# Raw inputs transposed ahead of their norm, with gains and row scales applied afterwards, in a two-layer decoder trunk

## The reference

```python
for i in range(2):
    h = rms_norm(x, attn_norm[i])
    x = x + (swa_sink_attention(h, ...) if i == 0 else stick_breaking_attention(h, ...))
    h = rms_norm(x, ffn_norm[i])
    x = x + (swiglu(h, ...) if i == 0 else moe_swiglu(h, ...))
return rms_norm(x, final_norm)
```

## Time and profile before

| | us |
|---|---|
| median of 3 runs | 1397.66 (1396.64 to 1399.08) |
| the profiled execution | 1399.92 |
| its span | 1398.10 |
| TensorE busy | 1379.1 (99%) |
| VectorE busy | 1091.6 (78%) |
| ScalarE busy | 922.9 (66%) |
| experts, from their first product | from 430.18 |

### The profile page before, as it was taken

The page is one execution under the profiler, slowest core; times in us unless marked ns, Lnnn a source line. Parts: engine busy times, 40 slices in busy tenths (PEclk is TensorE's granted clock), DMA queues, the critical chain, the costliest instruction groups (busy, mean ns, idle before and its releaser), DMA issues.

```text
span 1398.1 us, 19292 instructions
## 1 busy us (share of the span) xinstructions
PE 1379.1 (99%) x7165; PEld 1160.8 (83%) x7165; DVE 1091.6 (78%) x824; ACT 922.9 (66%) x762; POOL 43.3 (3%) x38
## 2 busy tenths in 40 slices
PE   9999999999999999999999999999999999999997
PEld 6879999889887888888888888888888888888885
DVE  5964444464548888988988898888888888889886
ACT  5754333445456777777777777777777777778775
POOL 2100000000000000000100000010000000000000
PEclk9999999999999999999999999999999999999999
DMA  9446553744327999999999999999999999999993
GB/s 324 156 162 206 190 181 122 247 159 158 114 91 292 385 368 358 389 387 371 369 394 374 353 395 389 359 376 394 380 349 394 386 361 373 390 372 359 392 372 124
DMA packets 185102, 430.48 MB, mean 308 GB/s; under 512 B 7047, under 2 KB 12241, under 8 KB 185058
## 3 DMA queue, kind: packets, MB, share of 16 engines
q1 hardware_dynamic: 181344, 417.36, 81.8%
q0 software_dynamic: 2896, 10.03, 2.6%
q10 hardware_dynamic: 818, 2.47, 0.6%
HBM read 422.48 MB, written 7.36 MB: 307 GB/s over the span
## 4 chain that ended last, share of the span: by engine, by line
PE 90%; DVE 5%; DMA 2%; issue 1%; ACT 1%; DVEq 0%; ACTq 0%; POOLq 0%
PE bank L1354 87%; DVE low L533 2%; DMA sum_dram<-qT,slot_row 2%; PE bank L1731 2%; DVE h L984 1%; PE bank L1700 0%; PE bank L1406 0%; PE bank L1515 0%; DMA qT<-in_onehot 0%; DVE work L1275 0%; DVE inT_low L1020 0%; DVE peak L1077 0%; DVE h L1067 0%; DVE work L1067 0%; DVE slot_spare L1281 0%
## 5 line engine op out<-in xcount | busy, mean ns | idle before, releaser
L533 DVE TENSOR_TENSOR low<-raw,high 128x2048 fp32r<-128x2048 f32 (+1 forms) x397 | 898.8, 2276 | 216.4 <-ACT high L528 214.2
L528 ACT CAST high<-raw 128x2048 fp32r<-128x2048 f32 (+1 forms) x397 | 754.8, 1903 | 298.5 <-PE bank L1354 295.2
L1354 PE MATMUL bank<-high,inT_high 128*128 128x512 f32 x1000 | 394.8, 395 | 4.4 <-DVE low L533 2.8
L1354 PE MATMUL bank<-high,inT_low 128*128 128x512 f32 x1000 | 389.9, 390 | 0.0
L1354 PE MATMUL bank<-low,inT_high 128*128 128x512 f32 x1000 | 389.5, 390 | 0.0
L1354 PEld LDWEIGHTS bank<-high,inT_high 128*128 128x128 f32 x1000 | 187.8, 188 | 45.7 <-DVE low L533 5.9
L1354 PEld LDWEIGHTS bank<-high,inT_low 128*128 128x128 f32 x1000 | 187.7, 188 | 39.9
L1354 PEld LDWEIGHTS bank<-low,inT_high 128*128 128x128 f32 x1000 | 187.9, 188 | 37.5
L1354 PE MATMUL bank<-high,hid_high 128*128 128x512 f32 x528 | 207.2, 392 | 0.0
L1354 PE MATMUL bank<-high,hid_low 128*128 128x512 f32 x528 | 205.7, 390 | 0.0
L1354 PE MATMUL bank<-low,hid_high 128*128 128x512 f32 x528 | 205.5, 389 | 0.0
(11 more groups left out here) (180 smaller groups left out, 644.2 us busy)
## 6 DMA issues: line engine op xcount, KB each, us to landing
raw<-in_moe_w_gate SPq DMA_DIRECT2D x112, 1024.0 KB, 7.0
raw<-in_moe_w_up SPq DMA_DIRECT2D x112, 1024.0 KB, 7.2
raw<-in_moe_w_down SPq DMA_DIRECT2D x112, 1024.0 KB, 6.9
raw<-in_sb_w_qkv SPq DMA_DIRECT2D x12, 1024.0 KB, 5.3
raw<-in_ffn_w_down SPq DMA_DIRECT2D x11, 1024.0 KB, 4.9
raw<-in_ffn_w_gate SPq DMA_DIRECT2D x10, 1024.0 KB, 5.7
raw<-in_ffn_w_up SPq DMA_DIRECT2D x10, 1024.0 KB, 5.1
raw<-in_swa_w_qkv SPq DMA_DIRECT2D x4, 1024.0 KB, 12.1
```

The lines of the kernel that those rows point to most:

```text
L528: nc.scalar.copy(high[n % SPLIT][:, :, 0:c], raw[r][:, :, 0:c]).then_inc(high_done, 1)
L533: nc.vector.tensor_tensor(low[n % SPLIT][:, :, 0:c], raw[n % RAW][:, :, 0:c], high[n % SPLIT][:, :, 0:c].bitcast(F32), ALU.subtract).then_ ...
L1354: return nc.tensor.matmul(out, lhsT, rhs, start=start, stop=stop, **kw)
```

## The change

The inputs of kv, of the dense layer and of q1 are now transposes of x itself. The gain, which by then lies along partitions, is multiplied in when the banks are evicted (`gained_part_high`, `gained_part_low`); the row scale is applied to the results: to k, v and q of layer 0, to the gate block ahead of Silu (up's factor is applied where the down product is added to x), and to q, k and v of layer 1. Where tokens lie along the free axis, the scales are spread over partitions by a matmul of ones with a diagonal. The transposes of each half of the features are issued as soon as x has that half, inside the products around; squares, roots and reciprocals follow behind them in `late_norm`. The last dense block is ordered by halves of the output. All gains and biases of the columns come in by three loads and one transpose. In `sb_sums` two matmuls become one.

```diff
@@ PSUM banks @@
-    transposed("hT1", (5, 0, 2, 1))
+    transposed("hT1", (5, 2, 3, 7))
+    u.use(("R", 1), 6)
@@ POOL @@
-            pool.dma_start(bias_tiles[:, :], a["swa_b_qkv"][0].rearrange("(t p) -> t p", p=P)).then_inc(biases_loaded, 16)
...
@@ ScalarE @@
+            act.dma_start(ident, a["consts"][:, C_IDENT:C_IDENT + P]).then_inc(ident_loaded, 16)
+            for r0, rows in ((0, a["swa_b_qkv"].rearrange("o (t p) -> (o t) p", p=P)),
+                             (QKV_TILES, a["attn_norm"].rearrange("l (t p) -> (l t) p", p=P)),
+                             (QKV_TILES + 2 * DT, a["ffn_norm"].rearrange("l (t p) -> (l t) p", p=P))):
+                act.dma_start(column_rows[r0:r0 + rows.shape[0], :], rows).then_inc(rows_of_columns_loaded, 16)
             act.dma_start(rel[:, :], a["rel_bias"]).then_inc(rel_loaded, 16)
             act.dma_start(onehot, a["onehot"]).then_inc(rel_loaded, 16)
-            act.dma_start(first_gain, a["attn_norm"][0:1]).then_inc(gain_loaded, 16)
-            act.dma_start(consts[:, :], a["consts"]).then_inc(consts_loaded, 16)
+            act.dma_start(consts[:, P:C_COLS], a["consts"][:, P:C_COLS]).then_inc(consts_loaded, 16)
...
+            def late_norm(k, name, next_table):
+                added = lambda tb, dh: taken(act, (name, dh, tb))
+                for dh in range(DH):
+                    for tb in range(TB):
+                        added(tb, dh)
+                        squares(tb, dh)
+                    for j in range(2):
+                        gained_part_high(f"hT{k}", 2 * dh + j, gains[k])
+                nc.scalar.preload_act_table(ACT.Sqrt)
+                for tb in range(TB):
+                    square_root(k, tb)
+                nc.scalar.preload_act_table(next_table)
+
+            def gained_part_high(name, j, gain):
+                b = full(act, (name, j))
+                for s in range(2):
+                    t = 2 * j + s
+                    ins = nc.scalar.activation(inT_high[:, t, :], b[:, s * SEQ:(s + 1) * SEQ], ACT.Identity,
+                                               scale=gain[:, t:t + 1])
+                ins.then_inc(input_high_ready, 1)
...
-            norm(0, lambda tb, dh: act.wait_ge(x_loaded[tb], 16))
+            act.wait_ge(x_loaded[0], 16)
+            for dh in range(DH):
+                squares(0, dh)
+            taken(act, "columns")
+            for j in range(2):
+                gained_part_high("hT0", j, gains[0])
             split_to(0)
-            input_high("hT0")
+            for j in range(2, 4):
+                gained_part_high("hT0", j, gains[0])
+            split_to(AT["q0"])
...
             split_to(end("wo0") + 1)
-            norm(1, added("wo0"))
-            input_high("hT1")
+            late_norm(1, "wo0", ACT.Silu)
             split_to(end("wo0") + SPLIT)
...
-                        p = full(act, ("fg", b, c))
-                        freed(nc.scalar.activation(f_silu[:, c * HALF:(c + 1) * HALF], p, ACT.Silu), ("fg", b, c))
+                        taken(act, ("fg", b, c))
+                        cols = slice(c * HALF, (c + 1) * HALF)
+                        nc.scalar.activation(f_silu[:, cols], f_gate[:, cols], ACT.Silu).then_inc(silu_done, 1)
...
-            norm(2, added("fy"))
-            input_high("hT2")
+            late_norm(2, "fy", ACT.Copy)
@@ VectorE @@
+            def row_scales(k):
+                dve.wait_ge(sumsq_ready, TB * DH * (k + 1))
+                V.tensor_tensor(total_sq[:, :], sumsq[:, :, 0], sumsq[:, :, 1], ALU.add).then_inc(total_sq_ready, TB)
+                dve.wait_ge(root_ready, TB * (k + 1))
+                steps.mark(V.reciprocal(rstd[:, k, :], root[:, :]))
+                steps.settle()
+                V.tensor_tensor(diagonal, ident.unsqueeze(1).to_broadcast([P, TB, P]),
+                                rstd[:, k, :].unsqueeze(2).to_broadcast([P, TB, P]), ALU.mult).then_inc(diagonal_ready, 1)
...
+            def late_norm(k, name, scales=(None, None)):
+                for dh in range(DH):
+                    for tb in range(TB):
+                        add_to_x((name, dh, tb), tb, dh, scale=scales[tb])
+                    for j in range(2):
+                        gained_part_low(f"hT{k}", 2 * dh + j, gains[k])
+                row_scales(k)
...
             def queries(j):
                 b = full(dve, ("q", j))
+                steps.mark(V.tensor_tensor(qT[:, 2 * j:2 * j + 2, :], b.rearrange("p (t s) -> p t s", t=2),
+                                           by_token(spread), ALU.mult))
+                steps.settle()
                 for s in range(2):
                     t = 2 * j + s
-                    ins = V.tensor_scalar(qT[:, t, :], b[:, s * SEQ:(s + 1) * SEQ], biases[:, t:t + 1], SCALE,
-                                          ALU.add, ALU.mult)
+                    ins = V.tensor_scalar(qT[:, t, :], qT[:, t, :], biases[:, t:t + 1], SCALE, ALU.add, ALU.mult)
@@ TensorE @@
+            pe.wait_ge(ident_loaded, 16)
+            pe.wait_ge(rows_of_columns_loaded, 48)
+            b = begin(pe, "columns")
+            filled(nc.tensor.transpose(b[:, 0:COLUMNS], column_rows[:, :], ident[0:COLUMNS, 0:COLUMNS]), "columns")
             pe.wait_ge(rel_loaded, 32)
...
-            pe.wait_ge(gain_loaded, 16)
-            for dh in range(DH):
-                filled(mm(begin(pe, ("gain", dh)), ones[0:1, :], first_gain[:, dh * HALF:(dh + 1) * HALF], True, True),
-                       ("gain", dh))
-            warm_up(1)
...
-            pe.wait_ge(consts_loaded, 16)
-            transposed_h(0)
+            for tb in range(TB):
+                pe.wait_ge(x_loaded[tb], 16)
+                for t in range(DT):
+                    turned("hT0", tb, t)
+            arrive("hT0")
...
-            by_tokens("wo0", AT["wo0"], (lambda: swa_transpose(2), last_values, None, None))
-            transposed_h(1)
+            by_tokens("wo0", AT["wo0"], (lambda: swa_transpose(2), last_values, None, None),
+                      lambda: turned_half("hT1", 0, "wo0"))
+            arrive("hT1")
...
                     by_features([("f" + kind[0], b, c) for c in range(2 if b < FFN_BLOCKS - 1 else 1)],
-                                AT[("ffn", kind, b)])
+                                AT[("ffn", kind, b)], None,
+                                (lambda: turned_half("hT1", 1, "wo0")) if first else None,
+                                (lambda: scales_spread(1)) if first else None)
...
-                    mm(b[:, 0:SEQ], tri, f[:, 0:SEQ], False, False, skip_group_check=True)
                     mm(b[:, P:SEQ], minus_ones[:, :], f[:, SEQ:SEQ + P], False, False, skip_group_check=True)
-                    ins = mm(b[:, SEQ:SEQ + P], tri, f[:, SEQ:SEQ + P], False, True, skip_group_check=True)
+                    ins = mm(b[:, 0:SEQ + P], tri, f, False, True, skip_group_check=True)
```

More of the change, by code:

```diff
@@ L169, in plan @@
     u.use("bias rows", 0)
-    for dh in range(DH):
-        u.use(("gain", dh), 1 + dh, counted=False)
+    u.use("columns", 7)
     for j in range(4):
         u.use(("hT0", j), 3 + j)
-    u.use("biases", 7)
     u.use(("kv", 0), 0)
+    u.use(("R", 0), 1)
     for n, bank in enumerate((1, 2, 7, 3)):
@@ L858, in _ @@
             split_to(end("v1") + SPLIT - 1)
+            for j in range(FT // 2):
+                taken(act, ("k1", j))
+            load_gain(3)
             for c in range(FT):
@@ L1026, in _ @@
+            b = full(dve, "columns")
+            freed(V.tensor_copy(columns[:, :], b[:, 0:COLUMNS]), "columns")
+            taken(dve, "columns")
             b = full(dve, "bias rows")
             freed(V.tensor_copy(bias_rows, b[0:H, 0:2 * WINDOW]), "bias rows")
-            norm(0)
+            for j in range(2):
+                gained_part_low("hT0", j, gains[0])
             split_to(0)
-            input_low("hT0")
-            split_to(1)
-            b = full(dve, "biases")
-            freed(V.tensor_copy(biases[:, :], b[:, 0:QKV_TILES]), "biases")
@@ L1034, in _ @@
-            taken(dve, "biases")
+            for j in range(2, 4):
+                gained_part_low("hT0", j, gains[0])
+            split_to(AT["q0"])
+            row_scales(0)
             dve.wait_ge(sinks_loaded, 16)
@@ L1123, in _ @@
             input_part_low("oT0", 3)
-            norm(1, "wo0", end("wo0") + 1)
-            input_low("hT1")
+            split_to(end("wo0") + 1)
+            late_norm(1, "wo0")
             split_to(end("wo0") + SPLIT)
@@ L1148, in _ @@
                     ffn_low(b + 1)
-            norm(2, "fy")
-            input_low("hT2")
+            late_norm(2, "fy", [rstd[:, 1, tb:tb + 1] for tb in range(TB)])
             split_to(end(("ffn", "down", FFN_BLOCKS - 1)) + SPLIT)
@@ L1451, in by_tokens, with by_features @@
                             between[n - n0]()
-            def by_features(keys, n0, between=None):
+            def by_features(keys, n0, between=None, middle=None, behind=None):
```

(13 more changed lines are left out.)

243 lines of the change are left out of this document (141 added, 102 removed).

## The result

The changed kernel takes **1412.30 us** (median, 1411.09 to 1413.81) against 1398.37 for the kernel before on the same chip (1396.64 to 1399.85): ratio 1.0099, 95% interval 1.0084 to 1.0114. It is slower, as forecast, but by 13.9 us and not by 4.3, and it lies outside the range. It is 1.5 less than the medians' 13.9 because the profiled execution of before, 1399.92, is one of its longest, while that of the changed kernel is at its median.

The account below looks back on a forecast made before the run. TensorE's issue was taken to set the time. Start +1.2, first passage +2.1, second -1.2, clock +2.6 and sums -0.4 gave +4.3 on the median 1397.66, so 1402 us, range 1395.5 to 1407.

Parts of the forecast that it names:

- The start: Up to the first wo0 product: later transposes and a longer VectorE queue, +1.2 us, bounds -1.0 to +3.5.
- Rival C: Start: small loads land later still and first products run at half speed; 3.5 instead of 1.2, 1404.3 us; chance 0.12.
- the 0.4 for the clock: Start: first products may find a slow clock after 2.6 idle us; 0 to 1.7 us, taken 0.4.
- First passage: wo0 to the dense layer: TensorE stands 5.8 us for gate's second unit, stage 2.1 us slower.
- 1.3 of clock: Behind each passage's stall: clock falls to half for at most 3.3 us, 1.65 lost; 1.3 taken each, +2.6 together.
- Second passage: Dense layer to q1: same stall, 5.8 or 4.5 us; -1.8 or -0.5, middle -1.2 taken.
- the -0.5 end: Passage from dense layer to q1: preload of Copy issues a table load, stall 5.8 us, stage -0.5.
- Rival D: Both stalls: a table load shuts ScalarE's queue for its length once more, 3.8 to 5.1 us, 1406.3; chance 0.03.
- Sums: Sums over keys: same columns, one instruction fewer per half head; -0.4 us, bounds 0 and -1.6.
- Hidden: Dense layer: gate eviction on VectorE stays under up's products; up to 0.5 us if the last block's cover is gone.
- A: Both passages: the stalls come but the clock holds; +1.7 without the 2.6, 1399.4 us; chance 0.20.
- B: Both passages: second units ready when wanted, stalls and clock loss go; -9.3, 1388.4 us; chance 0.09.

Follow-up runs that it names:

- experiment 1: Changed kernel with the second unit of each passage's pair split between late_norm's two feature halves: 1400.36 us, ratio 1.0015 to the kernel before.
- experiment 3: Changed kernel with seven clock-keeping matmuls of 512 columns between first and second unit in both passages: 1408.80 us, ratio 1.0077 to the kernel before.
- experiments 4: Changed kernel without the Copy table preload behind the second late_norm: 1413.75 us, ratio 1.0111 to the kernel before.
- Experiment 2: Changed kernel with x's 16 transposes ahead of the columns' transpose and bias rows in TensorE's order: 1409.48 us, ratio 1.0084 to the kernel before.
- Experiment 7: Changed kernel with two spreading-matmul results, R(0) and R(2), moved to other PSUM banks: 1415.91 us, ratio 1.0122 to the kernel before.
- Experiment 9: The kernel of experiment 8 with ScalarE casting unit 5 ahead of its four toeplitz copies: 1394.33 us, ratio 0.9968 to the kernel before.
- experiment 10: The kernel of experiment 8 with 11 clock-keeping matmuls ahead of the first product: 1396.18 us, ratio 0.9987 to the kernel before.
- experiment 8: Changed kernel with early second-unit splits, x transposed first, no Copy preload and other banks for the spread scales: 1393.14 us, ratio 0.9968 to the kernel before.
- experiment 5: Kernel before with only the merged sums over keys (two matmuls become one): 1397.41 us, ratio 0.9994.
- experiment 6: Changed kernel with the rel and onehot loads issued ahead of ident and the column rows: 1412.48 us, ratio 1.0103 to the kernel before.

## Why the prediction was wrong

The direction was right, and in both passages the mechanism was. The start was not: it had terms at nothing and a wait that no sum held. By the prediction's own steps, in the profiled executions' numbers (12.4 measured, 4.3 forecast):

**The start is the step that failed most.** "Sum +1.2, bounds -1.0 to +3.5"; it measured +6.07, which is 4.9 of the 8.1 missing. Rival C had two of its causes, the late loads and the half-speed products, at 3.5 for the whole start; the wait for the cast is in no rival. Up to the biased scores the forecast, with the 0.4 for the clock, was 39.05 and the trace has 44.55. The 5.5 between are:
- 2.35: the first product at 18.00, not in the middle of 14.6 to 16.7. The step from transposes to product was right (6.1 forecast, 6.4 measured); the transposes started at 11.64 and not at 8.4 to 10.5. I took 7.4 us as the worst landing of a small load for onehot and got it (7.3), but averaged it with 4.2, and let the matmul of the bias rows cost nothing behind it: TensorE is on that from 10.68 to 11.64.
- 1.0: the first 96 products took 13.07 and not 11.64, 1.43 lost where I had taken 0.4. The bound of 1.7 held here, and not in experiments 1, 3 and 4 (2.2 to 2.6 with the same start).
- 0.2: the copy of the scales began 0.63 and not 0.45 behind the matmul's start.
- 1.85: VectorE idle for unit 5's cast, which ScalarE has behind the toeplitz copies. I summed VectorE's queue and never asked where ScalarE's stood.
- 0.1 in what is left: the queries took 3.6 instead of 2.8, and v and the k pieces gave that back, 1.7 instead of 2.4.

Behind the biased scores I took 1.2 for queries 2 and 3, and 0.5 came. Experiment 2 shows 3.8 us of the start to be TensorE's order. Experiment 7 shows that the bank wait cost the start nothing: a slower low part filled its place. Experiment 9 shows 1.1 behind the spreading matmul to be the order of ScalarE's casts, and experiment 10 shows 1.5 to be the clock. What stays in experiment 8 adds up from the cuts: 1.22 won by the first product, 1.74 lost by the 96 products, 1.99 from them to the biased scores and 0.54 behind, 3.05 in all. Of the 1.99 only experiment 9's 1.06 is isolated; the two-step eviction of the queries for what is left is argued.

**First passage, +2.1 and 1.3 of clock forecast, 3.9 measured.** The stall was 6.1 from the expected start (104.22 to 110.29), forecast 5.8, for the reason given; experiment 1 shows it by taking it away. The second transposes and the spreading matmul came 0.3 cheaper. The clock cost 2.0 (experiment 3), over my bound: I carried over the 3.3 us at half speed that followed a shorter idle time, and here it lasted 6.8, of which 4.4 were matmuls.

**Second passage, -1.2 and 1.3 forecast, +2.75 measured.** Three sizes were off. The Copy preload does load (the -0.5 end, 0.7 off). The clock cost 2.1 instead of 1.3. And 1.0 is a wait that I didn't look for: the result of the spreading matmul lies in the bank that the next unit needs. The 25.97 of before that this is counted from hold a fall of the clock themselves; from the 24.61 of experiment 5's trace, which has none there, the passage would be 4.1 slower. Rival D, the table load's length paid twice, is refuted: roots at 104.22 and casts at 106.01 follow each load at its end. The Trainium skill ("ScalarE: Activation LUTs", What ACT_TABLE_LOAD costs) counts 2.66 us for a switch with a drain; in this case's traces only 1.28 of it shows.

**Sums, -0.4 forecast.** Experiment 5 measures 0.9994 with 1 inside the interval, and the stage is 0.1 shorter in both traces: within the bounds of 0 and -1.6, and close to 0. The rest's -0.6 is something else: nearly all of it lies behind wo1, where the code is the same. **Hidden** work: +0.31 in the dense layer, inside the 0.5 named.

**Rivals.** A (the clock holds) is out, by the stretch at 0.50 behind each stall. B named 1388.4 as the time if the second units were ready; experiment 1 made them ready and gave 1400.4, since the start and the second bank wait stayed. Against 1412.3 that is 11.9 won, where the difference of forecast and B, 13.6, said what there was. C's late loads and slow products came, and its 1404.3 was still 8 short.

## What to carry to other kernels

When a norm moves behind the products that use its input, list what each engine has queued between the last operand of the old stage and the first of the new one, and put the split of the *second* unit ahead of it: that alone was worth 12 us here (both layers' splits together); the saved work of the first passage could give 3.9. Give a result that must be copied out before anything can use it a bank that the next matmul doesn't want. Price a stall with the clock behind it: about 6 us of idle time brought 6.8 us at half clock and 2.0 of loss, twice the length that a shorter one had brought. And at the start count every small load that TensorE's order puts ahead of the first transpose.

## What the runs showed of the hardware that I had not expected

**GpSimd and VectorE slow each other.** GpSimd's timeline in the changed kernel, beside VectorE's queries shown above:

```profile
37.82 1.08 POOL L671 TENSOR_SCALAR_AFFINE_SELECT kv_area<-work 128x1024 f32<-128x1024 f32 x1
38.87 3.14 POOL L668 TENSOR_SCALAR_AFFINE_SELECT kv_area<-work 128x1024 f32<-128x1024 f32 x1
```

A selection of this size takes 1.08 alone and 3.14 beside a low part (38.75 to 41.05). In the kernel before one and the same line shows both, and the low part beside the second (33.85 to 36.91) took 3.06 where 2.29 is its time alone:

```profile
32.63 1.09 POOL L663 TENSOR_SCALAR_AFFINE_SELECT kv_area<-work 128x1024 f32<-128x1024 f32 x1
...
34.72 3.14 POOL L663 TENSOR_SCALAR_AFFINE_SELECT kv_area<-work 128x1024 f32<-128x1024 f32 x1
```

In the changed kernel the query additions from SBUF take 1.55 and then 0.62; the multiplications, which read one operand from PSUM, take 0.68 in both places. The Trainium skill ("SBUF — State Buffer", SBUF: two separate sides) describes a pair of ports that VectorE, when it reads two SBUF operands or runs a fast mode, and GpSimd take from each other for a whole instruction; the traces agree in which instructions suffer.

**The same stage has the clock's fall in one trace and not in another.** In the router's stage, with the same code, there was no stretch at 0.50 in the kernels before and after, one of 3.4 us in experiments 5 and 8, and one of 6.8 in experiments 4, 7, 9 and 10; the rest of the span took 1093.4 to 1093.6 in the changed kernel and experiments 2, 3 and 6, which have none, and 1096.2 to 1097.1 with the long one. So up to 3.7 us can come in that belong to no edit, as in experiments 4 and 7. What decides it is not shown: experiments 8 and 9 reach the stage 0.1 us apart (407.39 and 407.29) and have 3.4 and 6.8.

**Small loads land by their place.** The same 32 KB took 4.2 us in the kernel before, 7.3 after and 4.0 in experiment 6, and 64 KB took 4.0 or 7.6, depending on what was issued ahead of them.
